# Expert matmuls of a MoE layer: gate/linear contraction in one phase, unit by unit, with both thirds of the weights released together

## The reference

```python
gu = xb @ w_gu[e] + b_gu[e]                  # 1024 -> 2048
g, lin = jnp.split(gu, 2, axis=-1)
g = jnp.minimum(g, 7.0); lin = jnp.clip(lin, -7.0, 7.0)
act = g * jax.nn.sigmoid(1.702 * g) * (lin + 1.0)
ys = act @ w_down[e] + b_down[e]             # 1024 -> 1024
```

## Time and profile before

| | us |
|---|---|
| median of 3 runs | 2426.13 |
| lowest and highest | 2425.0, 2430.72 |
| profiled execution, device time | 2432.23 |
| profiled execution, span on the core | 2430.5 |
| PE busy in the span | 2136.2 (88%) |
| stretch of the 47 items | 523.5 to 2399.4 |

### The profile page before, as it was taken

The page is one execution under the profiler, slowest core; times in us unless marked ns, Lnnn a source line. Parts: engine busy times, 40 slices in busy tenths (PEclk is TensorE's granted clock), DMA queues, the critical chain, the costliest instruction groups (busy, mean ns, idle before and its releaser), DMA issues.

```text
span 2430.5 us, 53256 instructions
## 1 busy us (share of the span) xinstructions
PE 2136.2 (88%) x21037; PEld 924.2 (38%) x21038; DVE 769.7 (32%) x2033; ACT 388.2 (16%) x866; POOL 440.6 (18%) x420
## 2 busy tenths in 40 slices
PE   3998989959998999999796799797898889989994
PEld 3443444424433343443343233333343333433342
DVE  6437554232222232222222222222222222222223
ACT  3044112211011111101011101101101111010112
POOL 2000030112222121221211111111121111122121
PEclk9999999969999999999898899898999989999997
DMA  9312224323464357436799997699787549944245
GB/s 337 121 39 104 104 113 164 105 93 123 132 242 163 96 189 286 147 110 237 251 366 369 401 398 277 247 388 356 270 317 264 204 167 406 360 132 160 88 162 166
DMA packets 142462, 525.82 MB, mean 216 GB/s; under 512 B 14672, under 2 KB 45376, under 8 KB 109664
## 3 DMA queue, kind: packets, MB, share of 16 engines
q1 hardware_dynamic: 111728, 470.39, 49.9%
q0 software_dynamic: 30704, 55.06, 10.2%
HBM read 493.02 MB, written 32.37 MB: 216 GB/s over the span
## 4 chain that ended last, share of the span: by engine, by line
PE 58%; DMA 19%; issue 9%; DVE 6%; SPq 2%; ACT 2%; POOL 2%; POOLq 1%; DVEq 0%; ACTq 0%
PE psum L1117 29%; PE psum L1143 12%; DMA acc_rows<-r,sidx_cur 10%; PE psum L1013 4%; PE psum L880 4%; DMA r<-hs_rows,idx_next 4%; DMA big<-in_exp_w_gu_dram 3%; PE psum L975 2%; PE psum L1084 1%; PE psum L1129 1%; DMA big<-in_w_in_dram 1%; PE psum L1071 1%; POOL r L594 1%; PE psum L922 1%; DMA big<-in_exp_w_down_dram 1%
## 5 line engine op out<-in xcount | busy, mean ns | idle before, releaser
L1117 PE MATMUL psum<-big,r 128*32 128x512 f32 x9152 | 1022.0, 600 | 23.5 <-DMA big<-in_exp_w_gu_dram 23.0
L1143 PE MATMUL psum<-big,r 128*32 128x256 f32 x9152 | 529.2, 385 | 17.2 <-issue 14.2
L1117 PEld LDWEIGHTS psum<-big,r 128*32 128x32 f32 x9152 | 286.5, 111 | 675.7 <-issue 632.0
L1143 PEld LDWEIGHTS psum<-big,r 128*32 128x32 f32 x9152 | 293.7, 111 | 227.6 <-issue 54.2
L587 POOL DMA_INDIRECT acc_rows<-r,sidx_cur x143 | 229.0, 1601 | 804.8 <-DMA acc_rows<-r,sidx_cur 435.6
L787 ACT ACTIVATE r<-r 128x256 f32<-128x256 f32 x143 | 59.4, 416 | 1252.7 <-DVE r L1626 1252.7
L594 POOL TENSOR_TENSOR r<-r 128x256 f32<-128x256 f32 x143 | 104.5, 731 | 647.9 <-ACT r L787 647.8
L1620 DVE TENSOR_TENSOR r<-psum,r 128x256 f32<-128x256 f32 x143 | 60.7, 425 | 505.3 <-PE psum L1117 505.3
L1636 DVE TENSOR_TENSOR r<-psum,r 128x256 f32<-128x256 f32 x143 | 60.8, 425 | 437.0 <-PE psum L1143 437.0
L1084 PE MATMUL psum<-ident,r 128*128 128x128 f32 x384 | 70.7, 315 | 129.1 <-DMA r<-hs_rows,idx_next 129.1
L880 PE MATMUL psum<-r,big 128*128 128x512 f32 x384 | 167.8, 597 | 1.5 <-DMA big<-in_w_in_dram 1.5
(11 more groups left out here) (233 smaller groups left out, 1122.5 us busy)
## 6 DMA issues: line engine op xcount, KB each, us to landing
big<-in_exp_w_gu_dram SPq DMA_DIRECT2D x256, 1024.0 KB
big<-in_exp_w_down_dram SPq DMA_DIRECT2D x128, 1024.0 KB
big<-in_ada_w_dram SPq DMA_DIRECT2D x12, 2048.0 KB, 12.9
r<-in_x_dram SPq DMA_DIRECT2D x16, 512.0 KB, 12.5
big<-in_w_in_dram SPq DMA_DIRECT2D x4, 2048.0 KB, 19.1
r<-in_exp_b_gu_dram SPq DMA_DIRECT2D x128, 64.0 KB
big<-in_w_out_dram SPq DMA_DIRECT2D x2, 2048.0 KB, 13.3
hs_rows<-r POOLq DMA_DIRECT2D x8, 512.0 KB, 3.2
```

The source lines that it names most:

```text
L1117: last = pe.matmul(psum[32 * j:32 * j + 32, u, :].rearrange("p (a n) -> p a n", a=2), izT[:, k, u * UNIT:(u + 1) * UNIT], rhs[:, :, 256 * ...
L1143: ins_ = pe.matmul(psum[32 * i:32 * i + 32, 4 + u % 2, 0:256], actT[:, u, h, 32 * j:32 * j + 32], down_slab(f)[:, 256 * i:256 * i + 256], ...
```

## The change

Steps 1 to 4 of PE's order become one phase. For each unit in turn, all eight slabs are contracted: G(0,0), G(0,1), G(1,0), G(1,1), then `transpose_act(0)`, G(2,0), G(2,1), `transpose_act(1)`, G(3,0), G(3,1), `transpose_act(2)`. Both `transpose_rows` of the next item stand behind this phase, together, ahead of down. The release inside G(0,1) is gone: SP waits for `freed[1]` before chunk 0 (down's first matmul of the expert's last item) and no more before chunk 4. `freed[2]` before chunk 8 stays. On ACT, `modulate(g+1, 0)` moves behind the sigmoids of all units, next to `modulate(g+1, 1)`. The same instructions run, in another order; one semaphore is gone.

```diff
@@ -309,7 +309,7 @@
-        freed = [sem(f"freed{c}") for c in range(3)]
+        freed = {c: sem(f"freed{c}") for c in (1, 2)}
@@ -443,8 +443,8 @@
                 for q in range(CHUNKS):
-                    if q % 4 == 0:
-                        sp_.wait_ge(freed[q // 4], done)
+                    if q in (0, 8):
+                        sp_.wait_ge(freed[1 + q // 8], done)
                     sp_.dma_start(chunk_tile(q), chunk_source(e, q)).then_inc(w_arrived[q], SEMW)
@@ -807,7 +807,6 @@
                 by_units(act, units, 1, second)
-                modulate(g + 1, 0)
 
                 def fourth():
@@ -819,6 +818,7 @@
                 by_units(act, units, 2, third)
+                modulate(g + 1, 0)
                 modulate(g + 1, 1)
@@ -1160,39 +1160,29 @@
                 gate_and_linear(0, 0)
-
-                def first_3():
-                    gate_and_linear(3, 0)
-
-                def first_2():
-                    gate_and_linear(2, 0)
-                    by_units(pe, units, 3, first_3)
-
-                def first_1():
-                    gate_and_linear(1, 0)
-                    by_units(pe, units, 2, first_2)
-
-                by_units(pe, units, 1, first_1)
-                pe.wait_ge(z2_drained, g + 1)
-                gate_and_linear(0, 1, release=freed[0])
-
-                def second_1():
-                    gate_and_linear(1, 1)
-
-                by_units(pe, units, 1, second_1)
-                transpose_rows(g + 1, 0)
-                transpose_act(0)
-
-                def second_3():
+                pe.wait_ge(z2_drained, g + 1)
+                gate_and_linear(0, 1)
+
+                def unit_1():
+                    gate_and_linear(1, 0)
+                    gate_and_linear(1, 1)
+
+                by_units(pe, units, 1, unit_1)
+                transpose_act(0)
+
+                def unit_3():
+                    gate_and_linear(3, 0)
                     gate_and_linear(3, 1)
                     transpose_act(2)
 
-                def second_2():
+                def unit_2():
+                    gate_and_linear(2, 0)
                     gate_and_linear(2, 1)
                     transpose_act(1)
-                    by_units(pe, units, 3, second_3)
-
-                by_units(pe, units, 2, second_2)
+                    by_units(pe, units, 3, unit_3)
+
+                by_units(pe, units, 2, unit_2)
+                transpose_rows(g + 1, 0)
                 transpose_rows(g + 1, 1)
                 down(0, 0, 4, release=freed[1])
```

## The result

The changed kernel takes 2635.56 us (median of 3, 2629.24 to 2641.74) against 2426.13: a ratio of 1.0856 (95% interval 1.0819 to 1.0892), 209 us slower. The direction was forecast; the size was not, as 2548 was predicted, with 2605 as the upper end. The profiled execution took 2629.24 us, with a span of 2627.5.

A forecast was written before the change was run, and what follows sets the result against it. PE was taken as the bound, busy 88% of the span, with 173 us of waits. Items at 1705 us plus 251 slab, 22 gather and 20 clock gave 1998, 122 more than 1876: 2548 us, 8-in-10 range 2485 to 2605.

The forecast's parts named there:

- The gather's wait: PE's wait at line 1084 for the next item's rows: 122 us before, forecast to fall to 22 us.
- rival of slabs in time: At changes of expert: slabs never late, gather covered, kernel faster at 2277 us; anything on that side got 5%.
- L: Time from the release at down of the last item to slab 7's landing; put at 25.5 us, bounds 22.8 and 27.
- the sum: Undisturbed item times plus forecast waits and clock loss over the 47 items: 1998 us, against 1876 before.
- the lateness of slab 7: Next expert's first item waits L - D - 6.05: 3.0 to 14.2 us by last item's units, 251 us in all.
- D: Time from the start of down to the next item's start: 16.4, 12.9, 9.3, 5.2 us for four to one units.
- Clock: PE at low clock after slab waits: 1.4 us after each of 14 one- or two-unit last items, 20 us; bounds 0 and 50.
- one-unit items that aren't the first of their expert: Six of the eight one-unit items, whose gather no longer runs beside chunks; forecast 16.8 us each.
- exposed chain: In one-unit items PE waits at `transpose_act(0)` for the whole chain of engines, 2.8 us, formerly hidden by the gather wait.
- Waits at the transposes in the first items: Forecast only as gather waits: 11.5 and 7.5 us in two short items behind four-unit ones, 22 us with 3 for others.
- four scatters at 8.1 us: Behind a four-unit last item, scatters beside chunks push the gather to 16.7 us into the item, landing near 25.
- second rival: Cold clock on top: each of 31 expert changes pays low clock, 102 us in place of 20, about 2630 us; 10%.

The follow-up runs named there:

- before_late_release: Kernel before the change, old order kept, but chunk 0 waits for the release at down and the release in G(0,1) is gone: 2470.4 us, ratio 1.0154 to before.
- after_early_release: Changed kernel, with slabs 0 to 3 released at the first matmul of the second half of an item's last unit: 2536.8 us, ratio 1.0432 to before.
- after_clock_fill: Changed kernel, with eight extra matmuls behind each of slabs 4, 5 and 6 in each new expert's first item: 2616.1 us, ratio 1.0732 to before.

## Why the prediction was wrong

**What held.** Items with their weights in place take their old time (46.0 and 24.4 us). Slab 7 is late in each of the 31 changes of expert, and that is most of the loss behind last items of one to three units; before_late_release and after_early_release show that it is the release together with the order. The gather's wait goes (11 us left, 22 forecast), and the one-unit items behind an item of their own expert take some 7.5 us less than before. The rival of slabs in time was far off: L is 25.9 to 27.6.

**What failed.** The items take 2079.6 us, 82 more than the 1998 of the sum. The cut of the first items gives the terms:

- *L, the lateness of slab 7: 273 us, forecast 251.* L was 25.5 in the sum; it is 26.2 in the item at 612.9 and 27.6 behind a one-unit item. The step that failed is the value of L, mis-sized by some 0.5 us behind last items of three and four units and by 1.3 and 1.8 behind those of two and one. Behind one-unit items the sum came near (118 us, forecast 114) by luck: L is 27.3 in the mean, but D is 6.6 and not 5.2 (6.3 was what the row at the low clock showed); the two errors all but cancel. Part of the longer L is the bias rows, for which I had put 0.9 us on top of a mean round: issued behind slab 7 they give back 1.6. L behind one-unit items stays longest even then (26.0 against 24.6 behind four-unit ones); whether that is the gather, which falls into the same time, was not tried.
- *Clock: 52 us, forecast 20.* I charged 1.4 us behind last items of one or two units only, with 50 us as the upper bound. It came behind last items of three and four units too, 1 us or more in 26 of the 31 first items; after_clock_fill takes 37 of the 52 away. Some 14 us more are in the six one-unit items that aren't the first of their expert: 18.4 to 20.0 us each, forecast 16.8, since after the 3.06 us at the exposed chain eight transposes take 1.94 us (1.04 at full clock) and down 4.02. That the chain's wait would cost clock wasn't in the sum.
- *Waits at the transposes in the first items: 33 us, forecast 22.* I had put all 22 at the gather. Nearly all came one step earlier, at the activation, since the product of unit 0 stands in the same queue of POOL as the gather. The sum had counted "four scatters at 8.1 us" for the gather and had taken the chain of engines in items of two or more units as free; the two together were the step that failed. It is more than a term: behind a four-unit last item PE gets nothing from slabs that are in time, since the activation isn't there (after_early_release), so the lateness of 3.9 us and this wait, which I would have added up, lie largely one over the other. Most of the 11 us come from first items of three and four units behind a four-unit item, such as the one at 612.9, which had no wait in the forecast.

These are 22 + 32 + 14 + 11 = 79 of the 82 us. The second rival, "cold clock on top", named 2630 us and the result is 2636, but its price, 102 us of clock alone, is more than the 66 that the clock took: it came out near the time partly for a reason it didn't have.

The one mechanism that no step and no rival named is POOL's queue as the next bound. In the changed kernel it is worth 28 us of waits; it matters more in what followed. With the early release, it took back half of the 215 us, as the product on DVE then shows. With the late bias and the filled waits the wait for the activation took back 33 of 48 and 16 of 37 us; that this too is POOL's queue is argued from the first case.

The Trainium skill's rule on slab-paced waits (TensorE: Matmul & The Clock Gate, section "HAM oscillation — how this bites in real kernels") is borne out here in its direction: eight records take 1.94 us at 798.7, in a paced first unit, and 1.07 at full clock. It isn't so at every slab: at 620.3, behind a wait of 1.82 us, they still take 1.07.

## What to carry to other kernels

With a single weight buffer, count two distances for each slab: from its release to its landing, and from its release to its next use. An order that contracts a whole unit at once moves the release of all slabs to the end and the use of all slabs to the start, and both shorten the same distance. When transfers get denser, look at every in-order queue that waits for other transfers (here POOL's scatters) and at all that is queued behind them, for a small product may be what PE then waits for. And a correction that is worth little alone may only have its gain hidden by the next queue: try it together with the one that clears that queue.

## What the runs showed of the hardware that I had not expected

- PE does more work in less time: 1488 added matmul records in its waits raised the granted clock from 0.912 to 0.943 and made the kernel 1.2% faster.
- Loads with rows of half the length (4 KB for the gate/linear chunks in place of 8 KB) took 19.7 us for eight slabs where the full ones took 27.6, behind the same one-unit item.
- The eight DMAs with 384 KB of bias rows would take 1 us by bytes at 402 GB/s. In the item at 784.5, where they stand ahead of slab 4, PE waits 4.0 us for that slab and 0.3 to 1.5 for the others; issued behind slab 7, they leave 1.6 us of that wait.
